# A hybrid decoder layer: the last activation sum, the gate tiles and the tails change place at the seam between recurrence and Strassen products

## The reference

```
xn = rms_norm(x) * g
proj = xn @ w_in   # x_lru, z_lru, q, k, v, z_gla, a_lo(16), gate_logits(2 x 1024)
branch A: conv(4) -> RG-LRU recurrence -> h;  y_a = (h * silu(z_lru)) @ w_lru_o
branch B: gated linear attention, 4 heads;    y_b = (norm(o) * silu(z_gla)) @ w_gla_o
merged = sigmoid(g_a) * y_a + sigmoid(g_b) * y_b
y = rms_norm(x + merged @ w_out)
```

## Time and profile before

| | us |
|---|---|
| three timed runs | 1124.37, 1125.41, 1125.49 (median 1125.41) |
| the profiled execution, its own time | 1125.5 |
| its span (first to last instruction) | 1123.8 |
| TensorE matmuls busy | 1104.9 (98%) |
| VectorE busy | 639.3 (57%) |
| ScalarE busy | 463.0 (41%) |
| GpSimd busy | 214.3 (19%) |

### The profile page before, as it was taken

One profiled execution on the slowest core, in us unless ns is written; L12 is line 12 of the kernel. 1 busy time (PEld: TensorE's weight loads), 2 busy tenths in 40 slices (PEclk: granted clock), 3 DMA queues, 4 the chain that ended last, 5 costly groups with the idle time before them and its releaser, 6 DMA issues.

```text
span 1123.8 us, 17818 instructions
## 1 busy us (share of the span) xinstructions
PE 1104.9 (98%) x7001; PEld 1071.2 (95%) x7001; DVE 639.3 (57%) x842; ACT 463.0 (41%) x643; POOL 214.3 (19%) x136
## 2 busy tenths in 40 slices
PE   8999999999899999999999999999999999999997
PEld 7999999998899999999999999999999999998886
DVE  6677889896645336645844764485473223343423
ACT  6444555566333325446445544654542111112211
POOL 5631222220211121111120111112012112110000
PEclk9999999999899999999999999999999999999999
DMA  7212222221432322102210310221056102432222
GB/s 222 69 39 68 74 71 75 64 58 66 116 113 80 118 80 76 40 20 80 76 37 23 112 39 19 80 75 37 24 207 226 54 22 94 159 117 71 96 103 76
DMA packets 99680, 92.00 MB, mean 82 GB/s; under 512 B 4392, under 2 KB 89256, under 8 KB 99640
## 3 DMA queue, kind: packets, MB, share of 16 engines
q1 hardware_dynamic: 90684, 82.41, 23.5%
q10 hardware_dynamic: 8956, 9.06, 2.5%
HBM read 69.86 MB, written 21.60 MB: 81 GB/s over the span
## 4 chain that ended last, share of the span: by engine, by line
PE 55%; issue 36%; POOL 4%; DVE 3%; ACT 1%; DMA 1%; POOLq 0%; ACTq 0%; SPq 0%; DVEq 0%
PE ps L664 15%; PE ps L665 15%; PE ps L666 15%; POOL wlo L608 3%; PE ps L832 3%; PE ps L833 3%; PE ps L834 3%; DMA ngb<-in_norm_g 1%; ACT tf L1265 0%; PE ps L691 0%; DVE hh L1720 0%; DVE xt L1619 0%; PE ps L1102 0%; PE ps L1101 0%; DVE xn L1609 0%
## 5 line engine op out<-in xcount | busy, mean ns | idle before, releaser
L664 PE MATMUL ps<-xn,whi 128*128 128x364 f32 (+1 forms) x1056 | 354.8, 336 | 1.2 <-DVE xn L1609 1.2
L666 PE MATMUL ps<-xn,wlo 128*128 128x364 f32 (+1 forms) x1056 | 346.2, 328 | 0.0
L665 PE MATMUL ps<-xn,whi 128*128 128x364 f32 (+1 forms) x1056 | 346.0, 328 | 0.0
L608 POOL TENSOR_TENSOR wlo<-raw,whi 128x1024 fp32r<-128x1024 f32 x60 | 162.8, 2713 | 646.8 <-ACT whi L1135 646.6
L664 PEld LDWEIGHTS ps<-xn,whi 128*128 128x128 f32 x1056 | 198.7, 188 | 3.5 <-issue 1.5
L665 PEld LDWEIGHTS ps<-xn,whi 128*128 128x128 f32 x1056 | 198.8, 188 | 0.2
L666 PEld LDWEIGHTS ps<-xn,wlo 128*128 128x128 f32 x1056 | 198.4, 188 | 0.0
L1135 ACT ACTIVATE whi<-raw 128x1024 fp32r<-128x1024 f32 x58 | 61.0, 1052 | 99.8 <-PE ps L666 92.9
L664 PE MATMUL ps<-act_s,whi 128*128 128x364 f32 (+1 forms) x192 | 62.9, 328 | 0.5 <-POOL wlo L608 0.5
L832 PE MATMUL ps<-tf,whi 128*128 128x272 f32 x192 | 56.7, 295 | 6.7 <-DVE u L1857 5.0
L665 PE MATMUL ps<-act_h,whi 128*128 128x364 f32 (+1 forms) x192 | 63.0, 328 | 0.0
(11 more groups left out here) (312 smaller groups left out, 2084.9 us busy)
## 6 DMA issues: line engine op xcount, KB each, us to landing
raw<-in_w_in SPq DMA_DIRECT2D x56, 512.0 KB, 4.1
branch_a_in<-keep SPq DMA_DIRECT2D x8, 546.0 KB, 3.5
hzs<-branch_a_in SPq DMA_DIRECT2D x8, 546.0 KB, 7.5
mal<-gate_a SPq DMA_DIRECT2D x8, 544.0 KB, 3.7
xt<-in_x_prompt SPq DMA_DIRECT2D x8, 512.0 KB, 7.8
st<-in_state_gla ACTq DMA_DIRECT2D x4, 1024.0 KB, 5.5
out<-st ACTq DMA_DIRECT2D x4, 1024.0 KB, 4.4
raw<-in_w_gla_o SPq DMA_DIRECT2D x8, 512.0 KB, 3.6
```

The source lines that it names most:

```text
L608: pool.tensor_tensor(wlo[:, c % 2], raw[:, c % 2], whi[:, c % 2].bitcast(F32), ALU.subtract).then_inc(s["lo_ok"], 1)
L664: pe.matmul(dst, wh, mh, start=first, stop=False)
L665: pe.matmul(dst, wh, ml, start=False, stop=False)
L666: return pe.matmul(dst, wl, mh, start=False, stop=last)
```

## The change

- T4's block sum and subtraction are emitted on VectorE directly behind the last recurrence, ahead of t_lo(T2) and between t_lo(T2) and S1. Both write x22, in place; T4's hi goes to slot 1 of region 0 (HI_AT) and its lo back into slot 0, onto x22. T_SUMS counts eight sums instead of six.
- The two gate tiles lie in `dec` and `wt` instead of gtile at o_work; gate_a(0) waits for the seventh tile's recurrence instead of the sums. These bytes are region 2's, so t_hi(T3) waits for both gate stores (ga_out).
- trow moves by one slot and no longer waits for the gate stores. Its four stores are issued by SyncE, behind gate store 1, and t_hi(T4) waits for them ahead of the loop of products.
- load_pair(1) waits for the last hz store only, and stands between the two gate stores.
- ScalarE's order: alo_first(0), form_hi(1), t_hi(T3), alo_first(1), form_hi(2), alo_first(2), t_hi(T4), then the loop. VectorE's t_lo(T4) stands between form_lo(3) and u2.
- wos and woraw begin at the next address that is 128 past a multiple of 1024, 320 bytes further on.

```diff
-T_SUMS = 6
+HI_AT = (0, 0, 0, 1)
+T_SUMS = 8
...
-        trow = at("trow", [NTAIL, D], F32, o_work)
-        gtile = at("gtile", [P, 2, TOK], F32, o_work)
+        trow = at("trow", [NTAIL, D], F32, o_work + HALF)
+        gtile = [dec, wt]
...
-        wos = at("wos", [P, 2, KT, D], F32R, o_work)
-        woraw = at("woraw", [P, D], F32, o_work + 2 * KT * D * 4)
+        o_wos = o_work + (P - base - o_work) % 1024
+        wos = at("wos", [P, 2, KT, D], F32R, o_wos)
+        woraw = at("woraw", [P, D], F32, o_wos + 2 * KT * D * 4)
...
+        def t_src(form):
+            return x22[:, :, :] if form == T4 else tsum[:, form]
+
+        def t_form(form, low):
+            return tf[:, REGION[form], HI_AT[form] ^ low]
...
             for i in range(2):
                 sp.wait_ge(s["ga_done"], i + 1)
-                sp.dma_start(gates["a"][i], gtile[:, i, :]).then_inc(s["ga_out"], 16)
-            sp.wait_ge(s["t_lo"], 4)
-            load_pair(1)
+                sp.dma_start(gates["a"][i], gtile[i][:, :]).then_inc(s["ga_out"], 16)
+                if i == 0:
+                    sp.wait_ge(s["hz_out"], 16 * KT + ONE)
+                    load_pair(1)
+            sp.wait_ge(s["tails_ok"], 2)
+            for dst, r0, nr in (...):
+                sp.dma_start(dst, trow[r0:r0 + nr, :]).then_inc(s["tails_out"], 16)
...
             def t_hi(form):
-                act.wait_ge(s["t_sum"], T_SUMS + (2 if form == T4 else 0))
-                act.activation(tf[:, REGION[form], 0], tsum[:, form], ACT.Copy).then_inc(s["t_hi"], 1)
+                act.activation(t_form(form, 0), t_src(form), ACT.Copy).then_inc(s["t_hi"], 1)
...
-            act.wait_ge(s["t_sum"], T_SUMS)
+            act.wait_ge(s["h_tail"], KT - 1)
             gate_a(0, bankA)
             act.wait_ge(s["h_tail"], KT)
+            act.wait_ge(s["t_sum"], T_SUMS - 2)
             t_hi(T2)
             t_hi(T1)
             gate_a(1, bankB)
             form_hi(0)
             act.wait_ge(s["tails_T"], 1)
-            act.wait_ge(s["ga_out"], 32)
             for n in range(2):
                 act.activation(trow[:, n * 512:(n + 1) * 512], ...)
-            act.wait_ge(s["tails_ok"], 2)
-            for dst, r0, nr in (...):
-                act.dma_start(dst, trow[r0:r0 + nr, :]).then_inc(s["tails_out"], 16)
             alo_first(0)
             form_hi(1)
+            act.wait_ge(s["ga_out"], 32)
+            t_hi(T3)
             alo_first(1)
-            t_hi(T3)
+            form_hi(2)
             alo_first(2)
-            form_hi(2)
+            act.wait_ge(s["t_sum"], T_SUMS)
+            act.wait_ge(s["tails_out"], 64)
+            t_hi(T4)
...
                     act.activation(halves2(t1[:, :]), acc["X"][0], ACT.Copy).then_inc(s["c_gate"], 1)
-                    if p == 0:
-                        act.wait_ge(s["tails_out"], 64)
-                        t_hi(T4)
...
+            dve.wait_ge(s["t_sum"], T_SUMS - 2)
+            x_block(x22[:, :, :], 1, 0)
             t_lo(T2, 1)
+            t_sum(T4, x22[:, :, :], tsum[:, T2], T_SUMS - 1)
             weight_sum(0, "S1")
...
                     if p == 0:
-                        dve.wait_ge(s["hz_out"], 16 * KT + ONE)
-                        x_block(tsum[:, T4], 1, 0)
-                        t_sum(T4, tsum[:, T4], tsum[:, T2], T_SUMS + 1)
+                        t_lo(T4, 4)
                 elif o == 2:
...
                     weight_sum(p, "S4")
-                    if p == 0:
-                        t_lo(T4, 4)
```

More of the change, by code:

```diff
@@ L231, in build @@
         tf = at("tf", [P, 4, 2, KH, HT], F32R, o_work)
-        trow = at("trow", [NTAIL, D], F32, o_work)
-        gtile = at("gtile", [P, 2, TOK], F32, o_work)
+        trow = at("trow", [NTAIL, D], F32, o_work + HALF)
+        gtile = [dec, wt]
+        assert NTAIL <= P and D * 4 <= HALF
         assert 4 * HALF <= KT * TILE and 3 * HT * 4 <= HALF and 4 * HT * 4 <= HALF and 2 * KT * P * 4 <= HALF
@@ L265, in build @@
         hzs = at("hzs", [P, KT, 2, TOK], F32, o_xn)
-        wos = at("wos", [P, 2, KT, D], F32R, o_work)
-        woraw = at("woraw", [P, D], F32, o_work + 2 * KT * D * 4)
-        assert o_work + 2 * KT * D * 4 + D * 4 <= nc.sbuf_usable_end - base
+        o_wos = o_work + (P - base - o_work) % 1024
+        wos = at("wos", [P, 2, KT, D], F32R, o_wos)
+        woraw = at("woraw", [P, D], F32, o_wos + 2 * KT * D * 4)
+        assert o_wos + 2 * KT * D * 4 + D * 4 <= nc.sbuf_usable_end - base
         mal = at("mal", [P, 2, TOK], F32, o_glaconst)
@@ L503, in _ @@
                 sp.wait_ge(s["ga_done"], i + 1)
-                sp.dma_start(gates["a"][i], gtile[:, i, :]).then_inc(s["ga_out"], 16)
-            sp.wait_ge(s["t_lo"], 4)
-            load_pair(1)
+                sp.dma_start(gates["a"][i], gtile[i][:, :]).then_inc(s["ga_out"], 16)
[3 more added lines that the diff above has]
+            sp.wait_ge(s["tails_ok"], 2)
+            for dst, r0, nr in ((out[2][0], 0, 1), (out[5][0], 1, NSEQ), (out[3][0, 0], T_C, HIST),
+                                (out[6][0].rearrange("b k w -> (b k) w"), T_C + HIST, NSEQ * HIST)):
+                sp.dma_start(dst, trow[r0:r0 + nr, :]).then_inc(s["tails_out"], 16)
             for p in range(NP):
@@ L825, in product @@
                             cols = slice(j * HP, (j + 1) * HP)
-                            mh, ml = tf[:, REGION[form], 0, k, cols], tf[:, REGION[form], 1, k, cols]
+                            mh, ml = t_form(form, 0)[:, k, cols], t_form(form, 1)[:, k, cols]
                         else:
@@ L1260, in gate_a @@
                 act.wait_ge(s["job_done"], N_GA + i + 1)
-                act.activation(p3(gtile[:, i, :]), slot3(b), ACT.Tanh, scale=0.5, bias=dvec[:, i, V_BMA:V_BMA + 1]).then_inc(s["ga_done"], 1)
+                act.activation(p3(gtile[i][:, :]), slot3(b), ACT.Tanh, scale=0.5, bias=dvec[:, i, V_BMA:V_BMA + 1]).then_inc(s["ga_done"], 1)
             def t_hi(form):
-                act.wait_ge(s["t_sum"], T_SUMS + (2 if form == T4 else 0))
-                act.activation(tf[:, REGION[form], 0], tsum[:, form], ACT.Copy).then_inc(s["t_hi"], 1)
+                act.activation(t_form(form, 0), t_src(form), ACT.Copy).then_inc(s["t_hi"], 1)
             def form_hi(f):
@@ L1294, in _ @@
             act.wait_ge(s["tails_T"], 1)
-            act.wait_ge(s["ga_out"], 32)
             for n in range(2):
                 act.activation(trow[:, n * 512:(n + 1) * 512], ps[0:NTAIL, 6 + n, :], ACT.Copy).then_inc(s["tails_ok"], 1)
-            act.wait_ge(s["tails_ok"], 2)
-            for dst, r0, nr in ((out[2][0], 0, 1), (out[5][0], 1, NSEQ), (out[3][0, 0], T_C, HIST),
-                                (out[6][0].rearrange("b k w -> (b k) w"), T_C + HIST, NSEQ * HIST)):
-                act.dma_start(dst, trow[r0:r0 + nr, :]).then_inc(s["tails_out"], 16)
             alo_first(0)
             form_hi(1)
+            act.wait_ge(s["ga_out"], 32)
+            t_hi(T3)
             alo_first(1)
-            t_hi(T3)
+            form_hi(2)
             alo_first(2)
-            form_hi(2)
+            act.wait_ge(s["t_sum"], T_SUMS)
+            act.wait_ge(s["tails_out"], 64)
+            t_hi(T4)
             def gated(p, block, name):
@@ L1331, in _ @@
                     if p == 0:
-                        act.wait_ge(s["t_sum"], T_SUMS + 2)
+                        act.wait_ge(s["t_sum"], T_SUMS)
                         act.wait_ge(s["t_lo"], 1)
@@ L1733, in t_sum @@
                 dve.wait_ge(s["t_sum"], after)
-                dve.tensor_tensor(tsum[:, form], left, right, ALU.subtract).then_inc(s["t_sum"], 1)
+                dve.tensor_tensor(t_src(form), left, right, ALU.subtract).then_inc(s["t_sum"], 1)
             def lru_step(i):
@@ L1792, in t_lo @@
                 dve.wait_ge(s["t_hi"], n)
-                dve.tensor_tensor(tf[:, REGION[form], 1], tsum[:, form], tf[:, REGION[form], 0].bitcast(F32), ALU.subtract).then_inc(s["t_lo"], 1)
+                dve.tensor_tensor(t_form(form, 1), t_src(form), t_form(form, 0).bitcast(F32), ALU.subtract).then_inc(s["t_lo"], 1)
             def weight_sum(p, name):
@@ L1853, in _ @@
                     if p == 0:
-                        dve.wait_ge(s["t_sum"], T_SUMS + 2)
+                        dve.wait_ge(s["t_sum"], T_SUMS)
                     else:
```

## The result

| | before | after |
|---|---|---|
| timed runs, median | 1125.45 (1124.37 to 1125.88) | 1116.41 (1115.77 to 1116.65) |
| profiled execution, its own time | 1125.5 | 1116.54 |
| its span | 1123.8 | 1114.8 |

The ratio is 0.992 [0.9903, 0.9937]: faster by 9.0 us. The forecast was 1118.2, so 1.8 us more was gained than foretold.

What follows compares the result with a forecast made beforehand. TensorE, busy 98% of the span, was taken as the bound. Product 3 starting 4.6 us earlier plus 2.7 us of clock gave 7.3 us: 1125.5 - 7.3 = 1118.2 us, range 1115.7 to 1121.2.

Steps and rivals of the forecast that it cites:

- Hole 1: TensorE's gap between products 0 and 1: 0.85 us instead of 1.9, product 1 starting at 276.0.
- Parts B and C: ScalarE: trow, no longer waiting for the gate store, at 266.1; T3's hi, waiting for both gate stores, at 271.0.
- Hole 2: TensorE's gap between products 2 and 3: 1.65 us instead of 5.15 (1.1 to 2.5).
- Part A: VectorE: T4's sum moved right behind the last recurrence; u2 ends at 283.6, product 3 starts at 283.75 instead of 288.32.
- the contention row: VectorE's profile row before: block sum L1730 took 2.92 us instead of 2.42 beside GpSimd; 0.5 more assumed ahead of u2.
- Rival 3: Before u2: T4's hi waits for the tails' stores, cancelling the 4.6 us and the clock's gain; 1123.5 to 1125.5, chance 0.06.
- Rival 4: Before product 1: gate store 1 lands late and holds T3's hi; landing at 280 gives 1128.6 us, chance 0.05.
- The clock: TensorE at products 3 and 4: no fall to 0.50 after the shortened gaps, 2.7 us gained in full.
- rival 1: TensorE near products 1 to 4: the clock falls all the same after two gaps within 8 us; 1120.9 us, chance 0.09.
- Part D: Gate tiles in dec and wt, gate_a(0) waiting for h_tail 7 instead of the sums: claimed 0 us.
- Part E: Output stage: weights 320 bytes further on claimed 0 us, with 0.4 us as the bound to either side.
- Rival 2: Output stage: the weights' place in memory matters, up to 7.8 us less over 416 matmuls; 1110.4 us, chance 0.04.

Runs made afterwards that it cites:

- The undone Part B: The changed kernel with trow on ScalarE waiting for both gate stores again, all else as changed: 1119.45 us, ratio 0.9957 against the kernel before.
- experiments on act_h: Timing only, the changed kernel with act_h's moving operand shifted against the stationary one; with eight distances, 0 to 224 bytes: 165.4 to 168.1 ns per matmul, 1115.94 us.

## Why the prediction was right, and where it was not

**Hole 1 (Parts B and C): right.** With the 0.89 us taken off, trow started at 265.97 (said 266.1), S1 ended at 269.23 (269.4), gate store 1 landed at 270.98 (270.9), T3's hi started at 271.01 (271.0), the last alo piece ended at 275.86 (275.85) and product 1 started at 276.00 (276.0). The choice between the two ends of the landing, 270.9 behind the loads, was right, and the stretched S1 too: 1.73 us instead of 0.70 beside GpSimd's 2.53 instead of 1.29. The Trainium skill, SBUF - State Buffer, Who interferes with whom, says that such a pair contends; the trace agrees.

**Hole 2 (Part A): right, short by a tenth.** u2 ended at 283.71 (said 283.6), product 3 started at 283.86 (283.75); T4's lo took the 2.92 us that the contention row foretold. Rival 3 is out: T4's hi, at 276.21, had no idle time ahead of it, so the tails' stores were not waited for. Rival 4 is out at 271.87, against a limit of 275.5.

**The clock: right.** It stayed at 1.0 after holes of 0.85 and 1.73 us, so rival 1 is out. The undone Part B shows the other side: a hole of 4.35 us was followed by 3.4 us at 0.50. (From 1112.9 on the clock was at 0.50, behind the last matmul, which started at 1108.46; before, from 1120.3. This costs nothing, but "no stretch of clock 0.50 before 1118" was badly put.) The seam in all: 7.11 us, said 7.3; the 2.7 us for the clock are what this profiled execution of the kernel before had paid, and the one with the weights moved alone had paid 2.1.

**Part D: right**, nothing waited for the gate tiles' new buffers but T3's hi.

**Part E: wrong, and by more than the whole miss.** "The cost per column does not depend on where the tile begins, so I take 0" is the step that failed, with its bound of 0.4 us: the moved weights gave 2.72 us, and both experiments on it alone agree (2.75 between the median with the weights moved alone and the 1124.89 of the kernel before beside it; 96.83 us again in the output stage with the weights back). The prediction's own sign for this, a changed rate of the output stage, came. The evidence was near enough (302 counts matmuls cut by the window's ends; from start to start it was 233.3 ns, not 232) but not evidence on this: 0.453 and 0.455 ns a column compared a stage of 512 columns at a bad distance with one of 364 columns, which show no such dependence (experiments on act_h). Equal costs in two stages told nothing of what each would cost elsewhere. The argument also looked at the moving operand by itself and modulo 1024; what counts at 512 columns is the distance between the moving and the stationary start, modulo 256. Rival 2 had the direction, with a chance of 0.04, and nearly three times the size (7.8 us): at the best distance a matmul still costs 226.7 ns. The Trainium skill, TensorE: Matmul & The Clock Gate, Back-to-back issue gap, gives N/2.4 + 2.5 ns, 215.8 ns for this width, as the gap of an isolated matmul, and about 131 ns for a stream with weight loads. This case's stream agrees with neither: no distance tried came below 226.7 ns.

**The rest** is the start: -0.89 us, from the waits of the first 25 us (product 0 started between 271.72 and 273.17 in the thirteen kernels here, whose first stages are the same; each was profiled once). A prediction summed against one profiled execution carries this much uncertainty. Forecast 7.3, measured 7.11 + 2.72 - 0.89: the seam was foreseen in its mechanism and size, but that the total came within 1.8 us owes something to luck, since the late start hid a third of what Part E gave.

## What to carry to other kernels

Where TensorE is bound, follow each of its waits to the operation that stands in front of the awaited one on its engine, and move that one into idle time before the seam; check then what the waiting instruction now queues behind (here the last 2.8 us lay in two such orders, and turning them round removed both holes). When two stages are compared to show that something doesn't matter, they must both be able to show it: same width, same kind of operands, and one of them in the other state. And for matmuls of 512 columns that each load their weights it is worth trying to begin the moving and the stationary operand at the same place modulo 256 bytes; other widths than 512 and 360 to 364 were not tried.

## What the runs showed of the hardware that was not expected

- Matmuls of 512 columns with their weight loads: 226.7 ns, once settled, when both operands begin at the same place modulo 256 bytes, 229.0, 232.4 and 233.3 when the moving one begins 64, 128 and 192 bytes further; 236.7 and 240.0 at 4 and 132 bytes. After a change of the distance it takes up to ten matmuls until the new rate holds. That the two reads get in each other's way is a guess; what in the chip does it was not shown.
- Matmuls of 360 to 364 columns cost 165.4 to 168.1 ns at eight distances, with no cheap one.
- Holes up to 2.0 us left the clock at 1.0. One of 4.35 us was followed by 3.4 us at 0.50. With one of 5.15 us the clock was at 0.50 for 6.8 us, from 0.9 or 2.1 us before the hole's end.
- A store of 546 KB landed 2.8 us after its issue with no transfer near on its queue, 3.5 us with 1 MB of loads issued right behind it, 4.2 us with a store ahead that was still under way, and 5.3 to 6.0 us with 1 MB of loads ahead.
